# Middle layers of a three-part network: 28 weight blocks per layer in seven-product form, the 31-tap convolution moved into PSUM and into their loop

## The chip, the cores and the metric

One core of a Trainium2 chip runs the whole program in one launch. The metric is the time of one execution on the device in microseconds (us), the median of three. Engines are named as the profile names them: PE (TensorE; PEld is its weight load), DVE (VectorE), ACT (ScalarE), POOL (GpSimd) and SP (the queue that issues the weight transfers). All data is float32, and a float32 product is two matmul instructions in the trace.

## What is computed

256 tokens of width 1024 pass through five layers in three parts (A, B: attention and a recurrent layer; L0, L1: the hybrid layers that the change touches; C: a retention and attention layer). A hybrid layer, cut to what matters:

```python
h = rms_norm(x, norm1_g)
proj = h @ w_in                                  # 1024 x 10312
q, k, v, iq, ik, iw, a_in, c_in, g_in = jnp.split(proj, IN_SPLITS, axis=-1)
q = partial_rope(rms_norm(q), *rope_attn); k = partial_rope(rms_norm(k), *rope_attn)
iq = partial_rope(iq, *rope_idx); ik = partial_rope(ik, *rope_idx)
y_attn = dsa_attention(q, k, v, iq, ik, iw) @ w_attn_out     # 64 keys chosen per token
a_val, a_gate = jnp.split(a_in, 2, axis=-1)
a = causal_dwconv(a_val * sigmoid(a_gate), conf_conv_w) + conf_conv_b   # 31 taps
y_conf = silu(layer_norm(a)) @ w_conf_out
c_b, c_c, c_x = jnp.split(c_in, 3, axis=-1)
y_sc = (c_b * causal_dwconv(c_c * c_x, sc_conv_w)) @ w_sc_out           # 3 taps
g = sigmoid(g_in)
x = x + (g[0] * y_conf + g[1] * y_attn + g[2] * y_sc) @ w_o
u = causal_dwconv(rms_norm(x) @ w_up, ffn_conv_w) + ffn_conv_b
x = x + (silu(u_gate) * u_val) @ w_down
```

## The kernel before, in words

Channels lie on the 128 partitions and tokens along the free dimension; a tensor of 1024 channels is 8 tiles of 128x256. All weights stream once from memory in blocks of at most 1 MB (1024 rows by 256 output columns) through a ring of two slots. SP issues the load of a block when the slot's last block has been used (`load`, L659 to L671). `stream_plan` (L62) lists the stages and their blocks; every engine's program walks through the same list by hand, and they meet at semaphores. Each engine works strictly in its written order.

A plain block (`halves`, L710) takes two PSUM banks of four "main" banks (0 to 3) and runs 16 products of a 128x128 weight tile with 256 token columns. ACT or DVE empties each bank.

A seven-product block (`fast_block`, L772) does the same work by a recursive 2x2 form: 7 x 4 products of 128x128 by 128 columns instead of 8 x 4. It needs four sums of activation tiles (`token_sums`, L2134, on DVE, once per input), and three combinations of weight tiles, made on POOL in three or four instructions per block (`mix`, L1656) and written to one of two "homes" in turn: h_res, and a region that `home_of` (L576) names. Its PE part has a first half from the raw slot ("x": three products, after which the slot's PE use ends), and a second half ("y": four products) that waits for each of POOL's results. SP reloads the slot only when POOL is done with it as well. ACT copies one product out (`first_product`, L1402), and DVE puts the result together (`unite`, L2099, five additions at L2108 to L2117). Block n uses main banks 0 and 1, block n+1 banks 2 and 3, and block n+2 must find the first pair freed by `unite`.

The order in a hybrid layer, before (L1058 to L1136 for PE): the first convolution input block plain (a0), the other six in seven-product form (a); then plain: q (4 blocks), kv (2), iq (2), ik (72 columns); the sums for the norms of q and k and the small products on ik (side banks 4 to 7); gates (12 blocks), with the spreading of the q and k norms (L886) after the eighth and the mean of the layer norm; cx0 and cx1 (8 blocks, input of the short convolution), the eight index products, cb (4 blocks). Then comes a loop over 8 heads (`causal_heads`, L602): logits, one block (conf 0 to 3, sc 0 to 3), the transposition of the probabilities, the output of the head before. Last come attn, o and the feed-forward blocks, almost all in seven-product form.

DVE in the same stretch, before: the 31-tap convolution in one go (L2187 to L2196, 248 instructions of 128x256, accumulators in SBUF, two tiles alternating), then the norm and rotation work, the layer norm (L2214 to L2222), index scores, eight rounds of the choice of 64 keys (L2249 to L2261), the mask; in the heads, `masked`, the short convolution and the gated sums (L2272 to L2298), `normalised`. POOL before is busy only where there are seven-product blocks, and in between it adds the layer norm's sums (L1690 to L1699).

## Time and profile before

| what | value |
| --- | --- |
| median of 3 runs | 2019.52 us (2018.4 to 2021.51) |
| the profiled execution's own time | 2019.41 us |
| its span, first to last instruction | 2017.6 us |
| PE busy | 2003.7 us, 99% |
| DVE, ACT, POOL busy | 1055.7 (52%), 403.7 (20%), 782.2 us (39%) |
| memory read | 294.35 MB, 146 GB/s |
| granted TensorE clock | 1.00 of full speed over the span |

The span is cut into instructions; a row of a timeline gives the start, the length, the engine, the line, the operation with its tiles, how many were merged, and in brackets the idle time before it with what ended it. Busy times of neighbours on one engine overlap a little, so the distance between starts is the true price of an instruction in a row of such ones. The L0 stretch from q to the last head lies at 323 to 634 us of the span, and that of L1 at 951 to 1262 us.

### The profile page before, as it was taken

How to read it: one execution, taken by the hardware profiler on the slowest of the kernel's cores; microseconds unless marked ns; L12 is line 12 of the kernel's file. 1: busy time of each engine (PE TensorE's matmuls, PEld its weight loads, DVE VectorE, ACT ScalarE, POOL GpSimd, SP SyncE). 2: the span in 40 equal slices, each digit the busy share in tenths (PEclk: the TensorE clock that was granted, in tenths of full speed). 3: DMA queues.
4: the chain of work that ended last, by engine and by line, in shares of the span. 5: the costliest groups of instructions: out<-in, count | busy, mean ns of one | idle time of the engine just before them, and what ended most of it. 6: DMA issues, size and time to landing. Idle time of an engine off the chain costs nothing. (4 is left out here: it accounts for less than half of the span.)

```text
span 2017.6 us, 34732 instructions
## 1 busy us (share of the span) xinstructions
PE 2003.7 (99%) x13230; PEld 1836.6 (91%) x13230; DVE 1055.7 (52%) x2702; ACT 403.7 (20%) x986; POOL 782.2 (39%) x537
## 2 busy tenths in 40 slices
PE   9999999999999999999999999999999999999999
PEld 7788889888889999999888888999999999899998
DVE  4244446974343567514992454557823366555541
ACT  2231521112111222111122122032202014220000
POOL 1000042000002487765000000668875774248873
PEclk9999999999999999999999999999999999999999
DMA  5314444344334455444444433444454443345444
GB/s 209 128 45 144 146 149 148 132 152 146 132 140 142 151 170 169 172 146 161 134 147 150 146 128 123 170 165 168 162 173 148 145 147 105 126 146 183 171 159 136
DMA packets 42960, 298.32 MB, mean 148 GB/s; under 512 B 4928, under 2 KB 6080, under 8 KB 8832
## 3 DMA queue, kind: packets, MB, share of 16 engines
q1 hardware_dynamic: 42560, 295.42, 42.7%
q8 instruction: 99, 1.62, 0.3%
q10 hardware_dynamic: 256, 0.92, 0.3%
q14 instruction: 45, 0.37, 0.1%
HBM read 294.35 MB, written 1.05 MB: 146 GB/s over the span
## 5 line engine op out<-in xcount | busy, mean ns | idle before, releaser
L708 PE MATMUL bank<-xn,ring 128*128 128x256 f32 (+2 forms) x3776 | 686.4, 340 | 0.5 <-DMA ring<-wstream 0.5
L708 PEld LDWEIGHTS bank<-xn,ring 128*128 128x128 f32 x3776 | 610.2, 190 | 69.0 <-issue 4.6
L708 PE MATMUL bank<-arena,ring 128*128 128x128 f32 (+2 forms) x3702 | 641.4, 328 | 4.3 <-DVE arena L1711 2.4
L708 PEld LDWEIGHTS bank<-arena,ring 128*128 128x128 f32 x3702 | 564.2, 191 | 62.3 <-issue 3.5
L708 PE MATMUL bank<-arena 128*128 128x128 f32 (+3 forms) x2264 | 298.1, 287 | 0.0
L708 PEld LDWEIGHTS bank<-arena 128*128 128x128 f32 (+1 forms) x2264 | 274.9, 192 | 9.3 <-issue 1.5
L708 PE MATMUL bank<-arena,h_res 128*128 128x128 f32 x1960 | 234.5, 276 | 1.9 <-POOL h_res L1676 1.2
L708 PEld LDWEIGHTS bank<-arena,h_res 128*128 128x128 f32 x1960 | 225.7, 192 | 4.5 <-POOL h_res L1676 2.4
L1711 DVE SCALAR_TENSOR_TENSOR arena<-arena,par (+2 forms) x536 | 214.6, 475 | 0.3
L1667 POOL TENSOR_TENSOR h_res<-ring 128x512 f32<-128x512 f32 x12 | 15.5, 1294 | 495.2 <-issue 363.0
L1672 POOL TENSOR_TENSOR arena<-ring 128x1024 f32<-128x1024 f32 (+1 forms) x70 | 167.0, 2385 | 89.7 <-DMA ring<-wstream 89.7
L1231 ACT ACTIVATE arena<-bank 128x256 f32 (+5 forms) x216 | 86.6, 402 | 524.2 <-PE bank L708 421.4
L1672 POOL TENSOR_TENSOR h_res<-ring 128x1024 f32<-128x1024 f32 (+1 forms) x65 | 150.3, 2313 | 66.9 <-DMA ring<-wstream 66.9
L2111 DVE TENSOR_TENSOR partial<-bank,p1c 128x128 f32<-128x128 f32 x125 | 36.0, 288 | 211.1 <-PE bank L708 211.1
L1406 ACT ACTIVATE p1c<-bank 128x128 f32<-128x128 f32 x125 | 34.0, 272 | 509.8 <-PE bank L708 509.7
L1640 POOL TENSOR_TENSOR sq<-sq 128x256 f32<-128x256 f32 (+1 forms) x45 | 33.4, 743 | 219.9 <-ACT sq L1265 170.4
L1676 POOL TENSOR_TENSOR h_res<-h_res,ring 128x512 f32<-128x512 f32 (+1 forms) x77 | 98.5, 1279 | 6.0
L1679 POOL TENSOR_TENSOR h_res<-ring,h_res 128x512 f32<-128x512 f32 (+1 forms) x77 | 98.3, 1276 | 6.0
L2108 DVE TENSOR_TENSOR bank<-bank,p1c 128x128 f32<-128x128 f32 x61 | 18.2, 298 | 146.2 <-ACT p1c L1406 144.4
L1679 POOL TENSOR_TENSOR arena<-ring,arena 128x512 f32<-128x512 f32 (+1 forms) x70 | 92.2, 1317 | 5.5
L1676 POOL TENSOR_TENSOR arena<-arena,ring 128x512 f32<-128x512 f32 (+1 forms) x70 | 90.8, 1297 | 5.5
L1696 POOL TENSOR_TENSOR arena<-arena 128x256 f32<-128x256 f32 x14 | 10.1, 725 | 213.1 <-DVE arena L1711 212.6
(224 smaller groups left out, 1624.6 us busy)
## 6 DMA issues: line engine op xcount, KB each, us to landing
ring<-wstream SPq DMA_DIRECT2D x264, 1024.0 KB, 4.8
ring<-wstream SPq DMA_DIRECT2D x16, 768.0 KB, 4.2
cst<-consts SPq DMA_DIRECT2D x1, 2488.0 KB, 14.7
h_res<-tokens SPq DMA_DIRECT2D x2, 544.0 KB, 5.3
out<-arena SPq DMA_DIRECT2D x4, 256.0 KB, 5.4
arena<-arena ACTq DMA_DIRECT2D x4, 160.0 KB, 3.8
ring<-wstream SPq DMA_DIRECT2D x2, 288.0 KB, 2.8
par<-params SPq DMA_DIRECT2D x1, 541.5 KB, 9.2
```

What stands on the lines that cost most here:

```text
L708: return pe.matmul(o, lhs, rhs, start=start, stop=stop, skip_group_check=True)
L1231: ins = act.activation(dst, psum[b][0:rows, 0:T], func, **kw)
L1406: act.activation(p1c[:, b // 2 % 2, :], psum[b][:, 0:P], ACT.Copy).then_inc(*e.step((key, "p1")))
L1640: pool.tensor_tensor(out=acc, in0=acc, in1=squares[:, j, 0:T], op=ALU.add).then_inc(*e.step(event))
L1667: pool.tensor_tensor(out=m[:, 0:size], in0=w[:, size:2 * size], in1=w[:, 0:size], op=ALU.subtract).then_inc(*e.step(("mix1", block)))
L1672: pool.tensor_tensor(out=m[:, 0:2 * size], in0=w[:, size:3 * size], in1=w[:, 0:2 * size], op=ALU.subtract).then_inc(*e.step(("mix1", block)))
L1676: pool.tensor_tensor(out=m[:, 2 * size:3 * size], in0=m[:, size:2 * size], in1=w[:, 0:size], op=ALU.add).then_inc(*e.step(("mix2", block)))
L1679: pool.tensor_tensor(out=m[:, 3 * size:4 * size], in0=w[:, 3 * size:4 * size], in1=m[:, 2 * size:3 * size], op=ALU.subtract).then_inc(*e.s ...
L1696: pool.tensor_tensor(out=sel[:, 0, :], in0=one, in1=ac[:, j, :], op=ALU.add).then_inc(*e.step(event))
L1711: return dve.scalar_tensor_tensor(out=out, in0=a, scalar=scalar, in1=b, op0=op0, op1=op1)
L2108: dve.tensor_tensor(view[:, 0, 0, :], x[:, 2 * P:3 * P], p1, ALU.add).then_inc(*e.step((key, "c11")))
L2111: dve.tensor_tensor(u2, y[:, 3 * P:4 * P], p1, ALU.add).then_inc(*e.step((key, "u2")))
```

## The change

In both hybrid layers, 28 plain blocks each become seven-product blocks: q 4, k 1, v 1, iq 2, gates 12, conf 4, sc 4. POOL, ACT and DVE get the parts of `mix`, `first_product` and `unite` for them. The taps of the 31-tap convolution are accumulated in PSUM (bank 4, `both_p`) and run in groups of 10 behind each `unite`; the last groups stand among the later steps. The spreading of the norms, the index products, the index scores, the layer norm's sums, the short convolution, the c_b product and the choice of keys are cut up and placed between single blocks of cx0, cx1 and cb. The c_b product reads PSUM in place of ACT's copy. POOL does the eight multiplications of x_res in L0 that DVE did. Side banks in this stretch are 5 to 7 only ("beside"). Two more products run at the very start of the program (8 for 6).

```diff
-        pl(n + "q", "w_in_2", l, 2, 2, 8, seq(qo))
-        pl(n + "kv", "w_in_2", l, 1, 2, 8, seq(ko))
-        pl(n + "iq", "w_in_2", l, 1, 2, 8, seq(iqo))
+        fast(n + "q", "w_in_2", l, 4, 1, lambda it, q: qo + 256 * it)
+        fast(n + "k", "w_in_2", l, 1, 1, lambda it, q: ko)
+        fast(n + "v", "w_in_2", l, 1, 1, lambda it, q: vo)
+        fast(n + "iq", "w_in_2", l, 2, 1, lambda it, q: iqo + 256 * it)
...
-        pl(n + "g0", "w_in_2", l, 3, 2, 8, seq(go))
-        pl(n + "g1a", "w_in_2", l, 1, 2, 8, seq(go + 1536))
-        pl(n + "g1b", "w_in_2", l, 2, 2, 8, seq(go + 2048))
+        fast(n + "g", "w_in_2", l, 12, 1, lambda it, q: go + 256 * it)
...
-        pl(n + "conf", "w_conf_out_2", l, 2, 2, 8, seq(0))
-        pl(n + "sc", "w_sc_out_2", l, 2, 2, 8, seq(0))
+        fast(n + "conf", "w_conf_out_2", l, 4, 1, lambda it, q: 256 * it)
+        fast(n + "sc", "w_sc_out_2", l, 4, 1, lambda it, q: 256 * it)
...
+        if kind == "beside":
+            self.turn["side"] += self.turn["side"] % 4 == 0
+            kind = "side"
...
-            for n in range(6):
+            for n in range(8):
                 mm(7, slice(0, P), slice(0, S), sq[:, 8, 0:P], sq[:, 8, 0:S])
...
+                halves(L + "cx0", 0, 8, [P, P], x256, S)
+                spread(range(3))
+                halves(L + "cx0", 1, 8, [P, P], x256, S)
+                spread(range(3, 5))
+                halves(L + "cx0", 2, 8, [P, P], x256, S)
+                pe.wait_ge(*e.at((L + "ikr",)))
+                pe.wait_ge(*e.at((L + "iqr",)))
+                index_products(0, 3)
+                halves(L + "cx0", 3, 8, [P, P], x256, S)
+                index_products(3, 6)
+                halves(L + "cx1", 0, 8, [P, P], x256, S)
+                index_products(6, 8)
+                halves(L + "cx1", 1, 8, [P, P], x256, S)
                 centre_sums(L + "ln", 1, lambda j: sel[:, 0, :], [(L + "ln", "total")])
...
+                    fast_block((F, part, h % 4, 0), (F, part, h % 4, 0), of_tokens(buf), (F, sums),
+                               ready=[(L + "ys", j) for j in range(ND)] if h == 4 else None)
...
+                for it in range(12):
+                    first_product((F, "g", it, 0))
+                    if it >= 1:
+                        gate_tanh_l(it - 1)
...
+                    if L == "L0" and b == ("L0", "g", 11, 0):
+                        pool.wait_ge(*e.at(("N3", "inv")))
+                        for j in range(ND):
+                            pool.tensor_tensor(out=x_res[:, j, :], in0=x_res[:, j, :], in1=tmp[:, 2, 0:S],
+                                               op=ALU.mult).then_inc(*e.step(("N3", "xn", j)))
+                    if b[0] == L and b[1] == "g":
+                        for j in {3: (1,), 6: (2, 3), 11: (4, 5, 6, 7)}.get(b[2], ()):
...
+                def convolved(lo, hi):
+
+                    for n in range(lo, hi):
+                        j, k = 2 * (n // (2 * CK)) + n % 2, n % (2 * CK) // 2
+                        acc, weight = both_p[:, n % 2, :], G(g("conf_conv_w_2"), CK * j + k)
...
+                            dve.wait_ge(*e.at((L + "tap", j, k - 1)))
+                            stt(ac[:, j, :] if k == CK - 1 else acc, cp[:, j, k:k + S], weight, acc, ALU.mult,
+                                ALU.add).then_inc(*e.step((L + "ac", j) if k == CK - 1 else (L + "tap", j, k)))
+
+                for it in range(4):
+                    unite((F, "q", it, 0), qk0[:, 2 * it:2 * it + 2, :], 0)
+                    convolved(10 * it, 10 * it + 10)
...
+                for it in range(12):
+                    unite((F, "g", it, 0), sg[:, 2 * it:2 * it + 2, :], 0)
+                    if it < 11:
+                        convolved(90 + 10 * it, 100 + 10 * it)
+                convolved(200, 210)
+                spread_norm(L + "qk", range(3), lambda p: g("q_norm_g_2" if p < 4 else "k_norm_g_2"), qk0, qk0, L + "qkn")
...
+                scores(0, 3)
+                convolved(218, 228)
+                scores(3, 6)
+                convolved(228, 8 * CK)
+                scores(6, 8)
...
+                centred(L + "ln", 8, lambda j: ac[:, j, :])
+                dve.wait_ge(qk_halves, 32 * (l + 1))
+                rotate_in_place(qk0[0:32, :, :], qk[0:32, :, :], "attn", slice(0, 32), (L + "rotated",))
...
+                short_conv(1)
+                branch_b(0)
...
+                token_sums((F, "yc"), yc)
+                branch_b(1)
+                ranked(0, TOPK // 16)
+                branch_b(2)
+                ranked(TOPK // 16, TOPK // 8)
...
+                    unite((F, part, n, 0), both_p, 0, *([(F, "branch", h - 1)] if h > 1 else []))
+                    dst = mg[:, tiles, :] if h <= 4 else tmp[:, 0:2, 0:S]
+                    dve.wait_ge(*e.at((F, "sg", n + (0 if h <= 4 else 8))))
+                    stt(dst, gate, 1.0, both_p, ALU.add, ALU.mult).then_inc(*e.step((F, "branch", h)))
```

## Rows read from the trace of the kernel before

**Rows 1.** The page, busy time of PE in the span.
```profile
PE 2003.7 (99%) x13230; PEld 1836.6 (91%) x13230; DVE 1055.7 (52%) x2702; ACT 403.7 (20%) x986; POOL 782.2 (39%) x537
```

**Rows 2.** Timeline of PE in L0, plain blocks; start, length, operation, count.
```profile
444.36 4.48 PE L708 MATMUL bank<-tmp,cst 128*128 128x256 f32 x20
...
476.74 1.46 PE L708 MATMUL bank<-sq,cst 128*128 128x256 f32 x6
478.03 55.42 PE L708 MATMUL bank<-xn,ring 128*128 128x256 f32 x256
533.38 4.97 PE L708 MATMUL bank<-arena 64*128 64x128 f32 x32
```

**Rows 3.** Timeline of PE in L0's feed-forward part, two seven-product blocks' starts.
```profile
714.94 1.95 PE L708 MATMUL bank<-xn,ring 128*128 128x128 f32 x16
...
721.19 1.95 PE L708 MATMUL bank<-xn,ring 128*128 128x128 f32 x16
```

**Rows 4.** Timeline of PE in part C's heads, a seven-product block between logits and transposition.
```profile
1652.82 2.05 PE L708 MATMUL bank<-xn,ring 128*128 128x128 f32 x16
...
1659.18 0.49 PE L707 MATMUL bank<-cst,arena 128*128 128x128 f32 x3
```

**Rows 5.** Timeline of DVE in part C, one `unite` and what follows it.
```profile
1656.12 0.29 DVE L2108 TENSOR_TENSOR arena<-bank,p1c 128x128 f32<-128x128 f32 x1
1659.38 0.29 DVE L2111 TENSOR_TENSOR partial<-bank,p1c 128x128 f32<-128x128 f32 x1 [2.97 <-PE bank L708]
...
1660.99 0.62 DVE L1711 SCALAR_TENSOR_TENSOR arena<-bank,cst 128x256 f32<-128x256 f32 x2 [0.20 <-DVE arena L2117]
```

**Rows 6.** Groups by line and form: taps with SBUF and with PSUM accumulators; busy, mean ns.
```profile
L1711 DVE SCALAR_TENSOR_TENSOR arena<-arena,par x480 | 191.0, 474 | 0.3
...
L1711 DVE SCALAR_TENSOR_TENSOR bank<-arena,par,bank 128x256 f32<-128x256 f32 x176 | 73.0, 484 | 8.2 <-issue 8.2
```

**Rows 7.** Timeline of DVE: 60 taps in SBUF; 4 taps in PSUM beside POOL.
```profile
327.83 24.14 DVE L1711 SCALAR_TENSOR_TENSOR arena<-arena,par  x60
...
702.80 1.65 DVE L1711 SCALAR_TENSOR_TENSOR bank<-arena,par,bank 128x256 f32<-128x256 f32 x4
```

**Rows 8.** Timeline of POOL in L0's feed-forward part, one block's combinations.
```profile
728.77 2.41 POOL L1672 TENSOR_TENSOR arena<-ring 128x1024 f32<-128x1024 f32 x1 [0.95 <-DMA ring<-wstream]
731.26 1.28 POOL L1676 TENSOR_TENSOR arena<-arena,ring 128x512 f32<-128x512 f32 x1
732.62 1.29 POOL L1679 TENSOR_TENSOR arena<-ring,arena 128x512 f32<-128x512 f32 x1
```

**Rows 9.** The page's DMA issues, weight blocks: KB each, us to landing.
```profile
ring<-wstream SPq DMA_DIRECT2D x264, 1024.0 KB, 4.8
```

**Rows 10.** Timeline of DVE in L0, from centring to the first head.
```profile
450.00 2.77 DVE L2064 TENSOR_TENSOR arena<-arena,tmp 128x256 f32<-128x256 f32 x8
...
489.91 2.81 DVE L2051 TENSOR_TENSOR arena<-arena,cst 32x2560 f32<-32x2560 f32 x1
...
542.35 0.29 DVE L2255 MAX8 small<-tmp 128x8 f32<-128x128 f32 x1
...
552.28 0.61 DVE L1711 SCALAR_TENSOR_TENSOR arena<-arena,cst 128x128 f32<-128x128 f32 x2
567.00 0.29 DVE L1987 CUSTOM_DVE_ANT_0 arena<-bank,arena 128x128 f32<-128x128 f32 x1 [14.11 <-PE bank L708]
...
568.42 1.67 DVE L1711 SCALAR_TENSOR_TENSOR arena<-arena,par 128x256 f32<-128x256 f32 x4
```

**Rows 11.** Groups by line and form, then timeline of DVE in part C: both inputs in SBUF.
```profile
L2064 DVE TENSOR_TENSOR arena<-arena,tmp 128x256 f32<-128x256 f32 x24 | 17.3, 781 | 0.2
...
1661.53 2.10 DVE L1711 SCALAR_TENSOR_TENSOR arena<-arena 128x512 f32<-128x512 f32 x1
```

**Rows 12.** Timeline of PE at the start of the program.
```profile
1.11 5.49 PE L708 MATMUL bank<-sq 128*128 128x256 f32 x12 [1.11 <-POOL small L1624]
7.63 1.64 PE L708 MATMUL bank<-arena,ring 128*128 128x272 f32 x6 [1.03 <-DMA ring<-wstream]
```

More of the change, by code:

```diff
@@ L606, in causal_heads @@
             pts = probt3 if L == "C." else probt2
+            side = "side" if pair else "beside"
             def logits(h):
@@ L874, in unscaled, with row_sums @@
                            between=None if q else totals, late=2 if T == S and q == 0 else 0)
-            def row_sums(key, n, weights, per):
-                b = e.take("side", (key, "sum"))
+            def row_sums(key, n, weights, per, kind="side"):
+                b = e.take(kind, (key, "sum"))
                 pe.wait_ge(*e.emptied((key, "sum")))
@@ L1076, in _ @@
                 i0 = CONST["ident"][0]
[L1077 removed]
+                b = e.take("beside", (L + "iw",))
                 pe.wait_ge(*e.emptied((L + "iw",)))
@@ new lines, in index_products @@
+                def index_products(first, last):
+                    for i in range(first, last):
+                        t, j = i // 4, i % 4
+                        n, r, j2 = P * (t + 1), j // 2, j % 2
+                        rows = slice(64 * r, 64 * r + 64)
+                        b = e.take("beside", (L + "idx", t, j))
+                        pe.wait_ge(*e.emptied((L + "idx", t, j)))
+                        for s_ in range(2):
+                            ins = mm(b, slice(0, P), slice(S * s_, S * s_ + n),
+                                     iq0[rows, 2 * j2 + s_, P * t:P * t + P], ik[rows, 0, 0:n])
+                        ins.then_inc(*e.side_done((L + "idx", t, j)))
@@ L1386, in centred_squares @@
                     square(sq[:, first + j, 0:S], of(j), (key, "sq", j), (key, "c", j))
-            def gates(stage, first, its=3):
-                def body(i):
-                    for q in range(2):
-                        for t in range(2):
-                            out_of((stage, q, t), tile(sg, first + 4 * i + 2 * q + t), func=ACT.Tanh, scale=0.5,
-                                   event=(stage, "th", q, t))
-                if its > 1:
-                    with e.turns(stage, its) as i:
-                        body(i)
-                else:
-                    body(0)
             def first_product(key):
@@ L1457, in _ @@
-                gates(L + "g1b", 16, 2)
-                root((L + "ln", "var"), sq[:, 0, 0:S], D, RMS_EPS, (L + "ln", "rms"))
-                for j in range(8):
-                    act.wait_ge(*e.at((L + "z", j)))
-                    act.activation(ac[:, j, :], yc[:, j, :], ACT.Tanh).then_inc(*e.step((L + "zt", j)))
-                for c in range(2):
-                    with e.turns(f"{L}cx{c}", 2) as i:
-                        for q, dst in ((0, ys), (1, scp[:, :, 2:S + 2])):
-                            for t in range(2):
-                                out_of((f"{L}cx{c}", q, t), tile(dst, 4 * c + 2 * i + t), event=(f"{L}cx{c}", "in", q, t))
@@ L1467, in _, with gate_tanh_l @@
-                for t in range(2):
-                    n = P * (t + 1)
-                    for j in range(4):
-                        if (t, j) >= (0, 2):
+                def gate_tanh_l(it):
+                    for part in ("c11", "c12", "c22"):
+                        act.wait_ge(*e.at(((F, "g", it, 0), part)))
+                    act.activation(flat(sg[:, 2 * it:2 * it + 2, :]), flat(sg[:, 2 * it:2 * it + 2, :]), ACT.Tanh,
+                                   scale=0.5).then_inc(*e.step((F, "sg", it)))
@@ L2235, in _, with scores @@
-                dve.wait_ge(*e.at((L + "iws",)))
-                for t in range(2):
-                    n = P * (t + 1)
-                    score = tmp[:, t, 0:n]
-                    for j in range(4):
+                def scores(first, last):
+                    for i in range(first, last):
+                        t, j = i // 4, i % 4
+                        n = P * (t + 1)
+                        score = tmp[:, t, 0:n]
                         dve.wait_ge(*e.at((L + "rel", t, j)))
```

343 lines of the change are left out of this document (185 added, 158 removed).

## Prediction

> **What bounds the kernel now.** The page's busy times come first: PE is busy for 2003.7 us, 99% of the span [rows 1]. The question is therefore not where a wait can go, but how much PE work goes and whether everything that now has to keep pace with PE still does. PE's timeline gives the price of each kind of block. Eight plain blocks of 32 instructions take 478.03 to 533.38, 6.92 us each [rows 2]; a seven-product block in a steady series takes 714.94 to 721.19, 6.26 us [rows 3]. DVE's timeline shows how far it is ahead: the first head's logits are awaited for 14.11 us in L0 [rows 10], and 14.1 us in L1 by the same reading. That cover is what the change spends.
>
> **Step 1, 20 blocks before the heads** (q 4, k, v, iq 2, gates 12). Each loses 6.92 - 6.26 = 0.66 us: 13.2 us per layer. 28 products in place of 32 suggest 12.5%, but the rows show 9.6%: two 128-column instructions cost 0.223 us and one 256-column pair 0.432.
>
> **Step 2, 8 blocks in the heads.** In part C such a block lies between logits and transposition, and takes 1652.82 to 1659.18, 6.36 us [rows 4]. That makes 0.56 each, 0.66 if the extra tenth belongs to that part's logits. I take 0.6: 4.8 us per layer. Both layers: 2 x (13.2 + 4.8) = 36.0 us, bounds 35.4 and 37.0.
>
> **Step 3, POOL and the ring.** A block costs POOL 728.77 to 733.9, 5.1 us [rows 8], under PE's 6.26. A slot is reloaded after that and lands in 4.8 us [rows 9]; 9.9 us lies under the 12.5 us of two blocks, and the series of rows 3 runs just so without a gap. One addition of 0.72 us at gates 3, two at gate 6, a memset before q 0: all smaller than POOL's waits for the ring (0.95 us in rows 8). Cost taken 0; without that cover, the 1.2 us margin would have to go first. At gate 11 POOL does N3's eight products and waits for the last convolved tile; behind that wait stand only the squares' sums and conf 0's combinations. Conf 0's block lands after cb 2 has left the slot, some 12 us after it would be too early to mind: cb 3 takes 6.9 us, landing 4.8, and the split instructions are ready before the y half asks. Cost 0. ACT gets 28 short copies and 12 tanh; it is busy 20%, and its copies free banks well ahead. Cost 0.
>
> **Step 4, DVE inside the loop.** After y has ended, `unite` takes 1659.38 to 1660.99, 1.6 us, and L2108 before it 0.3 [rows 5]. Ten taps follow. With accumulators in SBUF they come every 24.14/60 = 0.40 us [rows 7]. In PSUM and beside a working POOL, the feed-forward taps are 484 ns long against 474 [rows 6], and four take 1.65, thus (1.65 - 0.48)/3 = 0.39 apart [rows 7]. A group costs 0.3 + 1.6 + 10 x 0.40 = 5.9 us, under 6.26. DVE waits for PE each time by 0.35 us, and no lag builds up. Cost 0, bounds 0 and what rival A gives. The Trainium skill speaks against this step (VectorE: DVE Perf Modes, section on the TRN2 errata): it states 120 fixed cycles for a PSUM source and 58 for an SBUF source at 0.96 GHz, thus 65 ns more per tap. By the page the group would be 6.5 us, as an estimate, and the total near 1990; the trace disagrees, with 10 ns more in the length and none in the spacing.
>
> **Step 5, DVE after the gates,** the step that decides. Time 0 is the end of gate 11 on PE. PE then needs 6 plain blocks (41.5), 5 spreads (4.5), 8 index products (5.0) and the mean's product (0.4) [rows 2], and reaches the mean at 51.4. DVE has by then: 48 taps (19.5), five products of 0.75 with a wait of 3.5 for the second lot of spreads, the index rotation (3.6), 16 score steps with their waits; it ends at about 48, and waits 3.5. From 51.4 it does not wait any more. Centring 3.2 (eight at 0.35 [rows 10]); rotation of q and k 3 x 2.8 = 8.4 [rows 10]; short convolution, half, 5.7 (eight taps at 0.40 as in rows 10 and the rest at 0.35 and 0.3); reciprocal 1.8; scaling 2.8; other half 5.7; cb product 0.8; gate of the branch 2.8; sums 2.8; keys and mask 10.5 (542.35 to 552.9 [rows 10]); three more cb products 2.3. The sum is 46.8, end at 98.2. The first softmax adds 2.4: 100.6. PE: 51.4 + 6 plain blocks 41.5 + 1.3 for the variance [rows 2] = 94.2, logits 0.7, conf 0 6.3: it asks for the probabilities at 101.2. The 14 us of cover have become 0.6 us. On the way there is one more meeting: cb 2 wants, at 80.4, the bank that DVE's first cb product frees at 79.8.
>
> What can make DVE late are operations with two SBUF inputs beside POOL: 2.10 us for one of 512 columns, which needs 0.69 alone, and 781 ns in the mean for those of 256, which need 0.42 [rows 11]. POOL's five sums for the variance run beside the first rotation, and conf 0's combinations (5.1 us) beside the keys. Bounds: nothing, and 2.2 + 4.7 = 6.9 us, if every key step doubled; less the slack, 0 to 6.3 us of stall per layer. I take 1.5, near the low end: four keys' rounds out of eight run beside POOL, and they read one SBUF tensor as the taps do, which were not lengthened [rows 6]. Both layers 3.0. The Trainium skill (SBUF — State Buffer, "Who interferes with whom") states that an instruction with two SBUF inputs and a POOL one that reads SBUF exclude each other for a whole instruction, and that one with a single SBUF input does not contend: by that rule the key steps cost nothing more and the stall is the rotation's, under 1 us; the total would be near 1985. Rows 11 and 6 agree with it.
>
> **Step 6, in the heads.** DVE per head: masking 0.9, `unite` 1.9, gate 0.7, second sum 0.7 to 2.1, normalising 0.8 to 1.1: 5.0 to 6.7 us against a block of 6.3. Only heads 5 to 7 have the second sum. Cost 0, upper bound 0.4 x 3 per layer, inside the margin above.
>
> **Step 7, the start.** The 12 early instructions take 5.49 us, 0.46 each, and end at 6.6; the first weights arrive at 7.63 [rows 12]. Four more end at 8.4: 0.8 us later, or 0.2 if the clock has come up by then, as the 0.27 of the next row suggests. I take 0.5, bounds 0 and 0.8.
>
> **Sum.** The profiled execution took 2019.41 us, within 0.1 us of the median. 2019.4 - 36.0 + 0.5 + 3.0 = 1986.9, thus 1987 us. All bounds best: 2019.4 - 37.0 = 1982.4. About 0.2% (4 us) is what a measurement of this kernel can tell from no change.
>
> **Rivals.** A, DVE is too slow in the loop (12%). If taps into PSUM did not overlap, they would be 0.48 apart; a group is 6.75 us, 0.49 over PE's, 9.8 us of lag in 20 blocks and 4 in the last 48 taps. The two waits of step 5 (7 us) take up half; 7 us of stall per layer remain in place of 1.5: 1987 + 11 = 1998. Against it: rows 6 and 7. For it: those were four taps in a row, not ten.
>
> B, the choice of keys comes late (14%). All the price of contention in step 5 is paid: 4.5 to 6.3 us per layer, 1993 to 1997. For it: the slack is 0.6 us out of 47 counted, and rows 11.
>
> C, slower than before (6%): the taps do contend with POOL. Place: the ten taps behind each `unite`, where POOL is busy 80% of the time while the old convolution had it idle. Price, by the mean of 0.78 us [rows 11]: a group of 9.7 us, 3.4 over PE's, 69 us in 20 blocks and 18 in the last 48 taps, less 7, thus 80 per layer: 2019 - 36 + 160 = 2143. It turns the sign when a tap costs over 0.53 us. Against it: the PSUM taps of rows 6 ran beside POOL at 484 ns.
>
> D, the ring does not keep pace (4%): with 0.5 us per block for landings, 28 us are given back, 2015 at worst. Against it: rows 3.
>
> Another 2% is left for no change that can be told.
>
> **How the numbers follow.** Forecast 62%, A 12%, B 14%, C 6%, D 4%, none 2%. Faster is the forecast with A, B and D: 0.92; same 0.02; slower 0.06. The range runs from 1981, just under the best sum, to 2000, which takes in A and B; C and most of D stay out.
>
> **What would show it.** Steps 1 and 2: blocks of 6.26 us on PE through q to gates, no idle time there. Step 4: DVE waits for PE at L2111's successor in each loop turn, with taps 0.40 apart; rival A shows none. Step 5: DVE's first masking follows the last cb product at once, with no wait for PE where 14.11 us stood, and PE is idle before the first transposition by 0 to 3 us; rival B more, with long rotation or key steps. Step 3: POOL's waits are for the ring. Wrong would be a PE block series above 6.3 us, or idle time of PE above 5 us per layer.

## The result and the profile after

The changed kernel takes **1994.32 us** (1992.78 to 1996.08, four runs) against 2019.07 in the same comparison (2018.40 to 2021.51). The ratio is 0.9875, 95% interval 0.9858 to 0.9893. It is faster by 24.8 us. The same kernel measured again later (e11 below) took 1992.98 us against 2020.83, faster by 27.9. The forecast was 1987 us, a gain of 32.5, with a range of 1981 to 2000. The profiled execution took 1992.78 us (span 1991.0), 26.6 less than the 2019.41 of before; the sums below are made on this pair.

The page's busy times first. PE stays at 99%, with 30 us less work; POOL has 294 us more [rows 1].

```profile
PE 1973.6 (99%) x14578; PEld 1851.5 (93%) x14578; DVE 1166.9 (59%) x2950; ACT 395.6 (20%) x972; POOL 1076.1 (54%) x717
```

Timeline of PE in L0 (start, length, operation, count, idle time before it): two blocks of q, then two heads.

```profile
323.68 1.95 PE L712 MATMUL bank<-xn,ring 128*128 128x128 f32 x16
...
329.94 1.95 PE L712 MATMUL bank<-xn,ring 128*128 128x128 f32 x16
...
582.14 2.84 PE L712 MATMUL bank<-arena,ring 128*128 128x128 f32 x24
...
590.03 1.95 PE L712 MATMUL bank<-arena,ring 128*128 128x128 f32 x16
```

A block is 6.26 us, as in [rows 3], where it was 6.92 [rows 2]. A head is 7.89 us; before, the same stretch took 8.55 (581.79 to 590.34). That is 0.66 per block in both places.

Timeline of DVE at the last gates, then the group of the taps by form (busy, mean ns), then DVE's waits (us, times, longest).

```profile
459.02 0.29 DVE L2151 TENSOR_TENSOR partial<-bank,p1c 128x128 f32<-128x128 f32 x1 [0.44 <-PE bank L712]
...
460.63 4.01 DVE L1751 SCALAR_TENSOR_TENSOR bank<-arena,par,bank 128x256 f32<-128x256 f32 x10 [0.20 <-DVE arena L2157]
```

```profile
L1751 DVE SCALAR_TENSOR_TENSOR bank<-arena,par,bank 128x256 f32<-128x256 f32 x640 | 259.5, 483 | 14.9 <-issue 7.5 <-DVE arena L2157 7.3
```

```profile
DVE partial L2151 <- PE bank L712: 240.6, 132, 4.2
```

Ten taps take 4.01 us, 0.40 apart and 483 ns long; that answers to rows 6 and 7. DVE waits for PE in each turn of the loop. No lag builds up there.

After the gates it looks different. Timeline of DVE in L0 from the mean to the first head:

```profile
510.95 0.42 DVE L2101 TENSOR_SCALAR tmp<-bank 128x256 f32<-128x256 f32 x1 [4.03 <-PE bank L712]
511.41 4.38 DVE L2104 TENSOR_TENSOR arena<-arena,tmp 128x256 f32<-128x256 f32 x8
515.71 3.34 DVE L2091 TENSOR_TENSOR arena<-arena,cst 32x2560 f32<-32x2560 f32 x1
518.98 3.33 DVE L2092 TENSOR_TENSOR arena<-arena,cst 32x2560 f32<-32x2560 f32 x1
522.42 2.81 DVE L2095 TENSOR_TENSOR arena<-arena 32x2560 f32<-32x2560 f32 x1
...
532.49 3.26 DVE L1751 SCALAR_TENSOR_TENSOR arena<-arena,par,sq 128x256 f32<-128x256 f32 x8
...
541.22 0.75 DVE L2327 TENSOR_TENSOR arena<-bank,arena 128x256 f32<-128x256 f32 x2
...
558.85 1.69 DVE L1751 SCALAR_TENSOR_TENSOR arena<-arena,cst 128x128 f32<-128x128 f32 x2
...
562.96 2.30 DVE L2046 TENSOR_SCALAR arena<-arena,small 128x128 f32<-128x128 f32 x2
```

Timeline of POOL in the same stretch: the five sums for the variance, and one addition of conf 0's and of the next block's combinations.

```profile
512.79 6.85 POOL L1675 TENSOR_TENSOR sq<-sq 128x256 f32<-128x256 f32 x5 [7.20 <-ACT sq L1259]
...
558.52 1.53 POOL L1711 TENSOR_TENSOR h_res<-h_res,ring 128x512 f32<-128x512 f32 x1
...
562.57 2.35 POOL L1707 TENSOR_TENSOR arena<-ring 128x1024 f32<-128x1024 f32 x1 [0.89 <-DMA ring<-wstream]
```

Centring takes 4.38 us where [rows 10] had 2.77, and the first two rotation steps 3.34 each where they had 2.81. All three run beside POOL's sums; the third rotation step, mostly after them, has its 2.81 again. The 14.11 us of cover in [rows 10] are gone. PE's timeline shows where that ends, in L0 and then in L1:

```profile
525.76 13.98 PE L712 MATMUL bank<-xn,ring 128*128 128x256 f32 x64
541.79 15.74 PE L712 MATMUL bank<-xn,ring 128*128 128x256 f32 x64 [2.05 <-DVE arena L2327]
...
565.32 0.55 PE L711 MATMUL bank<-cst,arena 128*128 128x128 f32 x3 [0.88 <-DVE arena L2046]
...
1156.64 15.74 PE L712 MATMUL bank<-xn,ring 128*128 128x256 f32 x64 [2.02 <-DVE arena L2327]
```

The same 64 instructions take 13.98 us in the first row and 15.74 in the second. Before the second, PE stood still for 2.05 us, waiting until DVE's first cb product had read its bank. The windows of L0 after that wait give the reason for the length (start and end, us, busy time of PE, PEld, DVE, ACT, POOL, then the granted clock, the DMA share and GB/s):

```profile
541.00:543.00 2.00, 1.21 (x5) 1.14 (x6) 2.00 (x7) 0.00 (x0) 0.00 (x0) 0.95 0.90 291
543.00:545.00 2.00, 2.00 (x6) 1.55 (x6) 1.87 (x6) 0.00 (x0) 0.00 (x0) 0.50 0.49 205
545.00:547.00 2.00, 2.00 (x8) 1.64 (x7) 1.93 (x4) 0.00 (x0) 0.00 (x0) 0.70 0.00 0
```

The granted clock falls to 0.50, thus to 1.2 of 2.4 GHz, about 1 us after PE has gone on, and stays there for some 3.4 us. That costs 15.74 - 13.98 = 1.76 us more. No such fall was inside the span of the profiled execution of before. So a stall at cb 2 cost 3.8 us in each layer of this execution, not 2.05. The fall doesn't come every time. In e11, the same kernel, the profiled execution has the same wait in both layers (2.04 us in L1) and no fall behind either. Its row in L0:

```profile
543.23 14.05 PE L712 MATMUL bank<-xn,ring 128*128 128x256 f32 x64 [2.05 <-DVE arena L2327]
```

14.05 is what the 64 instructions take behind such a wait at full clock, so the fall alone is worth 15.74 - 14.05 = 1.69 us.

**The ledger.** 20 blocks by 0.66 and 8 by 0.66 are 18.5 per layer, 37.0 in both. Taken off: twice 3.8 at cb 2, 0.9 at L0's first transposition, 0.4 per layer of short instructions after the gates (the mean is reached 51.8 us after gate 11 and not 51.4), 0.25 at the start. 37.0 - 7.6 - 0.9 - 0.8 - 0.25 = 27.5, where 26.6 was measured. Of the last 0.9 us, 0.4 are two blocks of L0 (v and the first of iq) that took 6.45 and 6.47 us; the rest we don't assign.

### The profile page after: what moved, and what is told of

It reads as the page before. It is cut to its first block and busy times, and to the rows that moved or that the text cites. A ratio compares the mean times of both kernels' runs of the same rounds, so it can differ in the third digit from the quotient of the medians.

```text
span 1991.0 us, 36677 instructions
## 1 busy us (share of the span) xinstructions
PE 1973.6 (99%) x14578; PEld 1851.5 (93%) x14578; DVE 1166.9 (59%) x2950; ACT 395.6 (20%) x972; POOL 1076.1 (54%) x717
## 3 DMA queue, kind: packets, MB, share of 16 engines
HBM read 294.35 MB, written 1.05 MB: 148 GB/s over the span
## 5 line engine op out<-in xcount | busy, mean ns | idle before, releaser
L712 PE MATMUL bank<-xn,ring 128*128 128x128 f32 (+3 forms) x3232 | 511.4, 314 | 4.1 <-DVE arena L2327 4.1
L712 PEld LDWEIGHTS bank<-xn,ring 128*128 128x128 f32 (+1 forms) x3232 | 460.3, 192 | 42.7 <-issue 9.2
L712 PE MATMUL bank<-arena 128*128 128x128 f32 (+5 forms) x2856 | 369.0, 285 | 0.0
L712 PEld LDWEIGHTS bank<-arena 128*128 128x128 f32 (+1 forms) x2856 | 343.0, 192 | 10.1 <-issue 2.8
L712 PE MATMUL bank<-arena,h_res 128*128 128x128 f32 x2600 | 310.7, 276 | 1.9 <-POOL h_res L1711 1.2
L712 PEld LDWEIGHTS bank<-arena,h_res 128*128 128x128 f32 x2600 | 299.4, 192 | 4.8 <-POOL h_res L1711 2.4
L1707 POOL TENSOR_TENSOR arena<-ring 128x1024 f32<-128x1024 f32 (+1 forms) x96 | 229.8, 2393 | 128.5 <-DMA ring<-wstream 128.2
L1707 POOL TENSOR_TENSOR h_res<-ring 128x1024 f32<-128x1024 f32 (+1 forms) x91 | 212.1, 2331 | 109.3 <-DMA ring<-wstream 92.9
L1751 DVE SCALAR_TENSOR_TENSOR bank<-arena,par,bank 128x256 f32<-128x256 f32 x640 | 259.5, 483 | 14.9 <-issue 7.5
L1253 ACT ACTIVATE arena<-bank 128x256 f32<-128x256 f32 (+6 forms) x120 | 50.1, 418 | 270.7 <-PE bank L712 184.5
```

The source lines that it names most:

```text
L712: return pe.matmul(o, lhs, rhs, start=start, stop=stop, skip_group_check=True)
L1253: ins = act.activation(dst, psum[b][0:rows, 0:T], func, **kw)
L1707: pool.tensor_tensor(out=m[:, 0:2 * size], in0=w[:, size:3 * size], in1=w[:, 0:2 * size], op=ALU.subtract).then_inc(*e.step(("mix1", block)))
L1751: return dve.scalar_tensor_tensor(out=out, in0=a, scalar=scalar, in1=b, op0=op0, op1=op1)
```

## Experiments

The theory after the result: the blocks gain what was forecast, and the rest is one chain. POOL's five sums lengthen DVE's centring and rotation; DVE's first cb product comes 2 us too late for cb 2; PE's idle time brings down its clock. Rivals: the fall of the clock has nothing to do with that wait; the order of DVE's pieces decides and not POOL; the wait only hides a later one at the first transposition. In the diffs below, "..." stands for lines left out, and the helpers' new parameters (`again`, `steps`) are not shown.

**e1: fill PE's wait.** Five products of cb 1's second tile are computed twice, before its own.

```diff
+                        if t == 1 and part == 0 and again:
+                            multiply(t, sum(widths[:t]), range(again))
                         multiply(t, sum(widths[:t]), ks)
...
-                    halves(L + "cb", q, 8, [P, P], x256, S)
+                    halves(L + "cb", q, 8, [P, P], x256, S, again=5 if q == 1 else 0)
```

> The changed kernel with five products computed a second time at the start of cb 1's second tile (2.2 us of PE work, no other effect), in both layers. PE then works where it sat idle for 2.05 us before cb 2. Theory (the idle time itself makes the granted clock fall, and the fall costs 1.75 us on top of the stall): cb 2 starts at the same time as in the changed kernel within 0.1 us, the 64 instructions of cb 2 and 3 take 13.98 us in place of 15.74, and no stretch at clock 0.5 is left; 3.5 us less than the changed kernel, 1990.8 us by the medians. Rival (the clock fall has another cause, or its stretch costs nothing that is not given back later): 15.74 us stays, time equal within 0.5 us.

Measured: 1990.43 us (1990.02 to 1993.23), ratio 0.985 (0.9834 to 0.9867). PE's timeline in L0:

```profile
527.05 30.08 PE L712 MATMUL bank<-xn,ring 128*128 128x256 f32 x138
```

128 instructions and ten repeated ones run without a gap, 0.218 us each, at full clock. In L1 it is the same (138 instructions in 30.05 us). PE did more work, and the median fell by 3.9 us, or by 2.6 against e11; 3.5 was expected. That the clock is the reason is read from the mean clocks. One fall takes 1.7 us of full clock out of some 1990, about 0.001 of the mean. The four executions of the changed kernel show 0.997 to 0.998, those of e11 0.998 to 0.999, those of e1 1.0 three times and 0.999 once. The one with 0.999 is the profiled one, and its fall is in part B, after another wait (e8 below). It took 1993.23 us, no less than the changed kernel's 1992.78, so a single pair of executions would not have shown the gain.

**e2: two cb products one place earlier.** DVE does the first cb product before the second half of the short convolution.

```diff
-                short_conv(1)
                 branch_b(0)
+                short_conv(1)
+                branch_b(1)
...
                 token_sums((F, "yc"), yc)
-                branch_b(1)
```

> The changed kernel with DVE's cb products 0 and 1 moved one place forward each: product 0 before the second half of the short convolution, product 1 right behind it. Same work, other order. Theory (cb 2 waits for a bank only because of where the first product stands, but DVE's total work up to the first softmax is the next limit): the wait of 2.05 us before cb 2 and the clock fall there are gone in both layers, but PE then waits for the first probabilities: 4.7 us in L0 (0.88 now) and 1.8 us in L1 (0 now). Net -2 us without a clock fall there, 0 to +1.5 with one. Rival (the bank was the only limit): both gains of 3.8 us per layer stay, -7.6 us, 1986.7.

Measured: 1995.78 us (1993.25 to 1996.09), ratio 0.9873 (0.9857 to 0.989). PE's timeline in L0:

```profile
527.23 27.79 PE L712 MATMUL bank<-xn,ring 128*128 128x256 f32 x128
...
564.74 0.75 PE L711 MATMUL bank<-cst,arena 128*128 128x128 f32 x3 [2.81 <-DVE arena L2046]
565.28 1.49 PE L712 MATMUL bank<-arena 128*128 128x128 f32 x4
```

The stall at cb 2 is gone, and the first transposition waits for 2.81 us (2.91 in L1; 4.7 and 1.8 were expected), again with a fall of the clock: the four instructions at 565.28 take 1.49 us where they take 0.82 at full clock. DVE has the same total to do before the first head, so a change of order only moves the wait. The median is 1.5 us above the changed kernel's, which the expectation gave for a wait with a fall; the rival's 1986.7 is refuted. The stall was not one of order at cb 2 alone: DVE is late in this stretch as a whole.

**e3: take three rotation steps out of the stretch.** q and k are rotated before the mean is awaited: the first step behind tap 228, the other two behind the last scores, where DVE otherwise waits for PE (1.95 and 4.03 us).

```diff
                 convolved(218, 228)
+                dve.wait_ge(qk_halves, 32 * (l + 1))
+                rotate_in_place(qk0[0:32, :, :], qk[0:32, :, :], "attn", slice(0, 32), (L + "rotated",), (0,))
                 scores(3, 6)
...
                 scores(6, 8)
+                rotate_in_place(qk0[0:32, :, :], qk[0:32, :, :], "attn", slice(0, 32), (L + "rotated",), (1,))
...
-                dve.wait_ge(qk_halves, 32 * (l + 1))
-                rotate_in_place(qk0[0:32, :, :], qk[0:32, :, :], "attn", slice(0, 32), (L + "rotated",))
```

> The changed kernel with DVE's rotation of q and k (three instructions of 2.8 us alone) moved ahead of the centring: the first behind the tenth-but-last lot of taps (228), the other two behind the last scores, where DVE waits 1.95 and 4.03 us for others. Theory (DVE's unfilled waits before the mean are what is missing after it): DVE reaches its first cb product some 6 us earlier, cb 2 starts at once, no clock fall, no wait before the first transposition: -8.5 us, 1985.8 by the medians. Rival 1 (what is moved forward delays the index scores and with them the last taps and the mean, so that all is given back): the mean comes 5 us later on PE, time as the changed kernel's or above. Rival 2 (the contention with POOL's five sums moves to other instructions of DVE): half the gain, -4.

Measured: **1987.16 us** (1986.44 to 1988.20), ratio 0.9835 (0.9819 to 0.9852). PE's timeline in L0, then DVE's:

```profile
527.05 27.79 PE L712 MATMUL bank<-xn,ring 128*128 128x256 f32 x128
...
561.58 0.49 PE L711 MATMUL bank<-cst,arena 128*128 128x128 f32 x3
```

```profile
515.37 4.37 DVE L2107 TENSOR_TENSOR arena<-arena,tmp 128x256 f32<-128x256 f32 x8
519.66 2.48 DVE L2314 TENSOR_TENSOR arena<-arena 128x256 f32<-128x256 f32 x4
...
538.67 0.75 DVE L2331 TENSOR_TENSOR arena<-bank,arena 128x256 f32<-128x256 f32 x2
...
559.18 0.53 DVE L2046 TENSOR_SCALAR arena<-arena,small 128x128 f32<-128x128 f32 x2
```

No wait at cb 2, none at the first transposition, in either layer of this execution. Centring still pays for POOL's sums (4.37), and the short convolution's first products now do too (2.48 for 1.41), but DVE is far enough ahead for cb 2. Counted from the start of cb 0 on PE, its first cb product comes 3.8 us earlier, not the expected 6: DVE reads the mean 2.7 us later than it did, and waits 1.79 us for ACT before the reciprocal. The expected 8.5 us were 7.2. The lead at the first transposition is about nothing, though: in other profiled executions with the rotation moved (e7 to e10, e12) PE waits there for 0 to 0.66 us, once for 1.20.

**e4: without POOL's sums.** The five additions of squares for the variance are left out of the computation, and PE's product for the variance reads the first square in place of their sum. The variance then lacks five of the eight squares.

```diff
-                for n, (event, j) in enumerate((((L + "ln", "acc"), 0), ((L + "ln", "sq", 6), 6), ((L + "ln", "sq", 7), 7))):
+                for n, (event, j) in enumerate((((L + "ln", "sq", 0), 0), ((L + "ln", "sq", 6), 6), ((L + "ln", "sq", 7), 7))):
...
-                        gather(L + ".ln", S, sq)
+                        pass
```

> The changed kernel without POOL's five additions of squares for the layer norm's variance, in both layers (the sum then lacks five of eight squares). Theory (these additions lengthen DVE's centring from 2.8 to 4.4 us and two rotations from 2.8 to 3.3 us, because both read two SBUF tensors): centring back at 2.8, rotation at 2.8 each, DVE 2.6 us earlier at its first cb product, so no wait before cb 2 and no clock fall. L1 gains 3.8 us, L0 2.6 us (it then waits 2 us before the first transposition): -6.4 us, 1987.9. Rival (these instructions are long for another reason, such as the tensors' places): 4.4 and 3.3 us stay, time unchanged.

Measured: 1987.93 us (1986.20 to 1988.75), ratio 0.9836 (0.982 to 0.9852). DVE's timeline in L0:

```profile
512.77 2.77 DVE L2104 TENSOR_TENSOR arena<-arena,tmp 128x256 f32<-128x256 f32 x8
515.46 2.81 DVE L2091 TENSOR_TENSOR arena<-arena,cst 32x2560 f32<-32x2560 f32 x1
...
539.91 0.74 DVE L2327 TENSOR_TENSOR arena<-bank,arena 128x256 f32<-128x256 f32 x2
```

Centring and both rotation steps have the lengths of [rows 10] again: 1.6 and 1.05 us per layer are POOL's doing. Cb 2 doesn't wait any more; 0.70 and 0.79 us at the first transposition remain. So these five additions, 2.7 us of DVE's time per layer, are enough to turn the meeting at cb 2.

**e5: the taps in SBUF.** The convolution of the loop accumulates in SBUF instead of PSUM, in the same places.

```diff
-                        acc, weight = both_p[:, n % 2, :], G(g("conf_conv_w_2"), CK * j + k)
+                        acc, weight = ac[:, j, :], G(g("conf_conv_w_2"), CK * j + k)
```

> The loop's taps accumulate in SBUF instead of PSUM: the operand alone is changed, in all 228 taps of a layer. The theory of rows 11 (an instruction with two SBUF inputs is held up by POOL's): the ten taps behind each unite run beside POOL's combinations, their mean goes from 0.48 us to between 0.6 and 0.78 and their spacing from 0.40 to 0.55 to 0.78, so a group of DVE takes 7.5 to 9.7 us against PE's 6.26, and PE waits in each block for its bank: 20 blocks by 1.2 to 3.4 us, less some 7 us of cover, per layer; the time is 2030 to 2143 us. The rival, that the taps would not have been held up in this place and PSUM is not what keeps step 4 free: spacing 0.40, no wait of PE in the blocks, 1992 to 1996 us.

Measured: **2095.7 us** (2093.41 to 2098.07), ratio 1.0369 (1.0353 to 1.0385): slower than before the change. The group of its taps, PE's largest wait, and DVE's and POOL's timelines in q's blocks:

```profile
L1751 DVE SCALAR_TENSOR_TENSOR arena<-arena,par 128x256 f32<-128x256 f32 x512 | 333.2, 721 | 7.8 <-DVE arena L2157 7.6
```

```profile
PE bank L712 <- DVE arena L2156: 60.5, 24, 5.6
```

```profile
346.60 7.23 DVE L1751 SCALAR_TENSOR_TENSOR arena<-arena,par 128x256 f32<-128x256 f32 x10 [0.20 <-DVE arena L2157]
...
355.55 4.05 DVE L1751 SCALAR_TENSOR_TENSOR arena<-arena,par 128x256 f32<-128x256 f32 x10 [0.20 <-DVE arena L2157]
...
361.31 11.30 DVE L1751 SCALAR_TENSOR_TENSOR arena<-arena,par 128x256 f32<-128x256 f32 x10 [0.20 <-DVE arena L2157]
```

```profile
345.61 2.35 POOL L1707 TENSOR_TENSOR h_res<-ring 128x1024 f32<-128x1024 f32 x1 [1.41 <-DMA ring<-wstream]
...
349.45 1.33 POOL L1714 TENSOR_TENSOR h_res<-ring,h_res 128x512 f32<-128x512 f32 x1
361.79 2.61 POOL L1707 TENSOR_TENSOR h_res<-ring 128x1024 f32<-128x1024 f32 x1 [11.02 <-PE bank L712]
```

These rows are worth reading side by side. From 350.8 to 361.8 POOL is idle, and the ten taps at 355.55 take 4.05 us. The ten before have POOL beside them for their first 4.2 us and take 7.23; the ten after have it beside them almost throughout and take 11.30. The instruction is the same, and so are its operands. PE waits 60.5 us for the banks (24 times, almost all of them in these blocks) and 9.7 for ACT at L1253 (no such wait in the changed kernel); and with the same 14578 instructions it is busy 2007.8 us in place of 1973.6, which fits the clock (its mean is 0.981, where it was 0.998). 60.5 + 9.7 + 34.2 = 104.4, of 105.3 between the two profiled executions. The choice of PSUM is thus what makes step 4 free. 2095.7 lies within the expected 2030 to 2143.

The Trainium skill (SBUF — State Buffer, "Who interferes with whom") states that a DVE instruction with two SBUF inputs contends with a POOL instruction that reads SBUF, and that the shared port pair is an exclusive lock. The lengths of e5 and e4 agree. It names `tensor_scalar` as another kind that can take the shared port; L2046's 2.30 us beside POOL in the changed kernel, 0.53 without it in e3, agrees too.

**e6: six early products, not eight.**

```diff
-            for n in range(8):
+            for n in range(6):
                 mm(7, slice(0, P), slice(0, S), sq[:, 8, 0:P], sq[:, 8, 0:S])
```

> The early products at the start go back from 8 (16 instructions) to 6 (12). The theory: they are off the path but for the 0.22 to 0.25 us by which the first block starts later; the time falls by 0.25 us, to 1994.1, which these rounds can't tell from nothing, and the page shows the first block at 7.63 again in place of 7.88. The rival, that the two more products keep TensorE's clock up through the first block's wait: the first blocks run longer than 4.39 us for the same instructions, or a fall of the clock appears early on, and the time rises by 1 us or more.

Measured: 1995.22 us (1992.74 to 1995.61), ratio 0.9872 (0.9856 to 0.9887), which can't be told from the change's own. First PE's start in the changed kernel, then in this one, with its cb 2:

```profile
1.10 6.56 PE L712 MATMUL bank<-sq 128*128 128x256 f32 x16 [1.10 <-POOL small L1659]
7.88 7.60 PE L712 MATMUL bank<-arena,ring 128*128 128x272 f32 x32 [0.22 <-DMA ring<-wstream]
```

```profile
1.10 4.72 PE L712 MATMUL bank<-sq 128*128 128x256 f32 x12 [1.10 <-POOL small L1659]
8.17 9.29 PE L712 MATMUL bank<-arena,ring 128*128 128x272 f32 x32 [2.34 <-DMA ring<-wstream]
...
545.98 14.05 PE L712 MATMUL bank<-xn,ring 128*128 128x256 f32 x64 [2.05 <-DVE arena L2327]
```

The first block begins when its weights land, at 7.5 to 8.2 us in these traces, whether 12 or 16 instructions ran ahead of it. Here that left a wait of 2.34 us, and the first block took 9.29 us in place of 7.60. And at cb 2 the same wait of 2.05 us as in the changed kernel was **not** followed by a fall: 14.05 us. So a wait of 2 us makes a fall possible and doesn't force it. The rival is not refuted. Its early fall of the clock is there in this execution, and the median is 0.9 us above the changed kernel's, inside the spread. The weights came latest here (8.17), and four more instructions would have shortened the wait before them. In e8, also with 12, the wait was 1.17 us and no fall came.

**e7: e3 and e2 together**, both diffs.

> The rotation moved ahead of the centring and the first two cb products one place earlier, together. The theory (after the rotation is moved no wait for DVE is left in this stretch, so nothing more can be gained): the same as with the rotation moved alone, 1987.2, within 1 us. The rival, that PE is still held up somewhere by the cb products or by the clock after them: 2 us or more less, 1985. The other rival, that the earlier products make the choice of keys late again: a wait of 0.3 us or more at the first transposition, 1988 to 1990.

Measured: 1987.57 us (1985.32 to 1988.22), ratio 0.9834 (0.9821 to 0.9847). The same as e3. Its first transpositions wait 0.59 us in L0 and 0.39 in L1, so the second rival has its wait, but the time doesn't show it; and e8 to e10, without the earlier products, have such waits too.

**e8: e3 and e6 together**, both diffs.

> The rotation moved and 6 early products: the version that should be the fastest. By the theory 1987.2 - 0.25 = 1986.9 us, ratio to the kernel before 0.9835, with no wait of PE at cb 2 or at the first transposition in either layer; if the early products matter by more than their length, 1988 or above.

Measured: 1988.36 us (1985.35 to 1989.34), ratio 0.9839 (0.9826 to 0.9853). The six products bring nothing. The median fits the rival, but the profiled execution, 1985.81, has no fall at the start or anywhere else in its span. It has no wait at cb 2, but one of 1.20 us at L1's first transposition (1171.83), where none was expected. The executions lie 4 us apart.

This spread draws attention to a wait that the kernel before has too: 2.42 us in part B, near 238 us, with a fall of the clock after it in the profiled executions of e1 to e7 (near 240 us), and none in those of before, after and e8.

**e9: e3, and that wait filled.** Eleven products of part B's last block of gates are computed twice.

```diff
+                            multiply(t, sum(widths[:t]), [k % 8 for k in range(again)])
...
-                        halves(stage, q, nk, [P] * tiles, rhs, T, ready=ready if q == 0 else None, token_major=q in token_major)
+                        halves(stage, q, nk, [P] * tiles, rhs, T, ready=ready if q == 0 else None, token_major=q in token_major,
+                               again=11 if (stage, q) == ("B.g1", 1) else 0)
```

> The rotation moved as before, and 11 products of part B's last block of gates computed twice (2.4 us of work in the place of PE's wait of 2.42 us at 237.7, which the kernel before has too). The theory (after a wait of 2 us or more the clock falls in some executions, for 1.7 us, and this is why single executions of one kernel lie in two clusters 2 us apart): no wait of PE is left at 240, the products cost nothing, and the clock's mean is 1.0 in every execution; the runs lose their upper cluster, the median is 1985.5 us, against 1987.2 with the wait. The rival, that the two clusters have another cause (landing of the weights, or the start): the times stay spread from 1985.3 to 1988.3 with a median near 1987. The other rival, that DVE needs the delayed bank: 1.5 to 2.4 us slower than with the rotation alone, 1989.

**e10: e3 once more**, and **e11: the changed kernel once more**, in the same comparison.

> The rotation moved, once more, beside the two others of this call: 1987.2 us again, its executions in two clusters near 1985.5 and 1987.5, with a mean clock of 1.0 in the lower and 0.999 in the upper; by the rival the clock and the time of an execution are not related.

> The changed kernel once more, beside the two others. The theory: four waits of 2 us or more, or of nearly 1, of which each can bring a fall of the clock, so 1992.5 to 1996 in steps of 1.7 us, median 1994.3; it lies 7 us over the rotated one. The rival, that the 7 us came from a difference between chips: less than 5 us apart here.

Measured: e9 1987.89 us (1986.70 to 1989.11), ratio 0.9837 (0.9823 to 0.9851); e10 1985.97 (1985.28 to 1989.12), 0.9832 (0.9819 to 0.9846); e11 1992.98 (1992.34 to 1995.15), 0.9866 (0.985 to 0.9882). PE's timeline of e9, then of e10:

```profile
223.34 18.73 PE L712 MATMUL bank<-xn,ring 128*128 128x256 f32 x86
241.90 10.31 PE L712 MATMUL bank<-arena,ring 128*128 128x256 f32 x47
```

```profile
239.80 12.54 PE L712 MATMUL bank<-arena,ring 128*128 128x256 f32 x57 [2.42 <-DVE arena L1751]
```

The rotation is worth 7.0 us beside e11 on the same chip, as it was between two chips (7.2): the rival of a difference between chips falls. In e9 the size of the filler was a mistake: a product is two instructions of 0.216 us, so 11 took 4.7 us and the next block began at 241.90, 2.1 later than in e10. All its executions show a mean clock of 1.0, but they still spread over 2.4 us, and e10's don't lie in two clusters (1985.97 with 0.999, 1986.94 with 1.0). The clock is not all that separates executions. The traces show short waits of PE that come and go: 0 to 1.2 us at the first transposition, 0.4 to 1.3 us before one feed-forward block in nine of the traces and none of 0.3 us or more in the others, and 0.7 to 1.65 us at one transposition of part C. What moves them is not shown.

**e12: the same with five products.** The diff is against e9.

```diff
-                               again=11 if (stage, q) == ("B.g1", 1) else 0)
+                               again=5 if (stage, q) == ("B.g1", 1) else 0)
```

> As the run with 11 products computed twice, but 5: each product is two instructions of 0.216 us, so 11 of them took 4.7 us and overran the wait of 2.42 us by 2.3 us; 5 take 2.2 us and fit. The theory (the clock's fall after this wait costs 1.7 us in the executions that have it): the wait is under 0.4 us, the mean clock is 1.0 in every execution, and the median is 1987.89 - 2.3 = 1985.6 us, 0 to 1.5 us under the kernel with the rotation alone. The rival (what separates the executions of one kernel is something else): no gain, 1986 to 1987.5, and still 2 us or more between the lowest and the highest execution.

Measured: **1985.27 us** (1984.93 to 1986.06, five runs), ratio 0.9829 (0.9815 to 0.9842), the lowest of all.

```profile
223.70 16.14 PE L712 MATMUL bank<-xn,ring 128*128 128x256 f32 x74
240.11 10.17 PE L712 MATMUL bank<-arena,ring 128*128 128x256 f32 x46 [0.28 <-issue]
```

The wait is 0.28 us, the clock 1.0 in every execution, and the spread 1.1 us against the 1.8 to 4.0 of e3, e7, e8 and e10. The median is 0.3 us under the theory's 1985.6. That the filler lowers the median of e10 (by 0.7 us) lies inside the intervals and is not shown: each is 34.9 us faster than the kernel before in its own comparison. The narrow spread fits all five executions, and five are few.

## Why the prediction was right, and where not

The time lies in the range, 7.3 us above the number (6.0 in e11). Faster was right for the reasons given. The profiled execution lies 5.9 us above the sum's 1986.9. Step 5 with the clock behind it gives 5.5 of that, the short instructions and the rest of the ledger 1.7, and steps 2 and 7 take 1.2 off, 6.0 by rounded terms.

**Step 1** held: blocks of 6.26 us, 13.2 per layer forecast. **Step 2**: 0.66 per block against the 0.6 taken; the other value named in the text was the right one, 1 us more in both layers. **Step 3** held: no wait of PE for the ring in q to gates. **Step 4** held: taps 0.40 apart, a wait of DVE for PE in each turn. The table of the Trainium skill (VectorE: DVE Perf Modes, the TRN2 errata) that spoke against it, from which 65 ns more per tap with a PSUM source were worked out as an estimate, is not borne out: 483 ns in PSUM, 474 in SBUF [rows 6], 0.40 apart in both.

**Step 5 failed in its size.** The 1.5 us of stall per layer became 4.2: 3.0 forecast for both layers, 8.5 measured in the profiled execution, 5.0 of it waits and 3.5 the clock behind them. In e11 the waits are 5.5 us (2.05 and 2.04 at cb 2, 0.65 and 0.80 at the first transposition) and no fall follows them. Three things went into that.

First, the place. The prediction put the stall at the first transposition and named the meeting at cb 2 (bank free at 79.8, wanted at 80.4) only on the way. Its own slack was the same 0.6 us there, and it comes 20 us earlier, so it breaks first. Measured from gate 11's end: bank wanted at 80.9, free at 83.0. Waiting there then let DVE catch up: at the first transposition 0.9 us were left in L0, none in L1 (0.65 and 0.80 in e11). e2 shows that the two places share one lag.

Second, what of DVE was long. The text gave POOL's sums to the first rotation step and took little for them. They began 1.4 us after the mean had been read, beside centring, and lasted 6.85 us: 1.6 us on centring, 1.05 on two rotation steps. e4 gives both back. In the prediction's terms, from the mean's product on PE to the free bank it counted 28.4 us, and 31.1 were measured: reading the mean and centring 5.1 for 3.2, rotation 9.5 for 8.4, scaling 3.2 for 2.8, all else 0.6 less. The scaling is no contention: POOL was idle then, and e4 has the same 3.26; it was priced 0.35 us apart and came 0.40 apart. What was feared, the key choice beside conf 0, didn't happen: MAX8 and MATCH_REPLACE8 kept 0.28 us (0.41 for 256 columns). But only the last two of the eight rounds ran beside POOL, not four. Behind them the mask and the normalising did grow, from 0.61 to 1.69 and from 0.55 to 2.30 us.

Third, the clock. The sum had no term for it. It is 1.7 us behind a stall of 2 us where it falls, 3.5 in the profiled execution, none at cb 2 in e11's and e6's, and e1 shows it apart.

**Step 7** took 0.5 us; the profiled execution shows 0.25, and e6, e8 and e11 (8.17, 7.75 and 7.62 for 7.88) show that the first block's start follows the landing of the weights. The products cost nothing that can be measured.

**Rivals.** A (taps 0.48 apart) fell with step 4. B had the right engine and the right cause (contention), too much of it, and not at the keys; its 1993 to 1997 holds the time, but that is luck: the time was reached by a stall at another place and by the clock. C is refuted for the kernel, but its mechanism is shown in e5: with the taps in SBUF it takes 2095.7, slower than before, where the text said 2143. D fell: PE waits 0.2 us for weights in all, at the start.

## To carry to other kernels

Where a change spends another engine's cover, list every place where the two engines meet, in order of time, with the slack of each; the first small slack decides, not the largest wait of the old profile. Price each DVE instruction that reads SBUF twice, and `tensor_scalar`, by what POOL does at that moment. And where PE is 99% busy, as here, count an idle time of 2 us as up to nearly twice its length: 3.8 us for 2.05 in some executions. A filler product in the gap gives the clock's part back (e1); work moved out of the chain that causes the gap gives both (e3). Since the fall comes in some executions only, compare several, and more than one profile.

## What the hardware showed that was not expected

The granted clock fell to 0.5 for some 3.4 us, within 1.4 us after PE had gone on, behind waits of 2.02, 2.05, 2.34, 2.42, 2.81 and 2.91 us. Behind the shorter waits of these traces, up to 1.65 us and in e5 up to 1.91, it did not; nor behind two longer ones in e5, of 2.61 and 2.79. The same wait can go either way. Of eight waits of 2.0 us at cb 2 (two each in the changed kernel, e5, e6 and e11) four had a fall; the 2.42 us in part B had one in eight traces of twelve. In e5, where waits follow closely on one another, falls also began while PE was still waiting, and the longest lasted 10 us. The Trainium skill (TensorE: Matmul & The Clock Gate, "The HAM clock gate") states that the clock's level is decided on a rhythm that doesn't start with the kernel, which would explain that one wait has both outcomes; no run here shows the rhythm itself.

One tap with both inputs in SBUF went from 0.40 to 1.13 us in the mean of ten beside POOL (11.30 for ten), while a tap with its accumulator in PSUM stayed at 0.40 beside the same POOL instructions.
